# The recurrence's chunk matrices as 64x64 blocks, and the triangular system by 16-blocks and an off-block part

## The reference

```python
def step(state, inp):
    r_t, w_t, k_t, v_t, aa_t, bb_t = inp
    sa = jnp.einsum('bhij,bhj->bhi', state, aa_t)
    state = (state * w_t[:, :, None, :] + sa[..., None] * bb_t[:, :, None, :]
             + v_t[..., None] * k_t[:, :, None, :])
    y = jnp.einsum('bhij,bhj->bhi', state, r_t)
    return state, y
...
xs = (r_h, w_h, k_h, v_h, -kk, kk * a_h)      # kk: k * k_k with each head at norm 1
yn = (y - mu) * lax.rsqrt(var + GN_EPS)       # per head, then gn_w, gn_b
bonus = jnp.sum(r_h * k_h * r_k, axis=-1, keepdims=True) * v_h
out = (yn + bonus) * heads(g)
```

## Time and profile before

| | us |
|---|---|
| device time, median of 3 runs | 3460.9 |
| lowest, highest | 3459.4, 3460.9 |
| span of the profiled execution | 3467.7 |
| the recurrence, units 0 to 7 (2032.6 to 2572.5) | 539.9 |

### The profile page before, as it was taken

How to read it: one execution, slowest core, us unless ns; L and a number is a source line. 1 busy time by engine, 2 the same in 40 slices (tenths; PEclk the granted TensorE clock), 3 DMA queues, 4 the chain that set the end, 5 groups by cost and what they waited for, 6 DMA issues and landing times.

```text
span 3467.7 us, 42391 instructions
## 1 busy us (share of the span) xinstructions
PE 3300.9 (95%) x16430; PEld 2572.9 (74%) x16430; DVE 2089.3 (60%) x3506; ACT 1468.8 (42%) x2635; POOL 0.2 (0%) x4
## 2 busy tenths in 40 slices
PE   8989999999999999999999998898999999999888
PEld 7456666788888877788886677787874788777766
DVE  3535766567666567755555766655544466655665
ACT  2213555553333345533335544444421464554333
POOL 0000000000000000000000000000000000000000
PEclk9999999999999999999997999999999999999999
DMA  6510000232333465433333000000022524455645
GB/s 258 182 43 1 1 1 13 73 104 82 94 114 105 149 215 177 151 110 103 116 100 134 16 19 7 13 26 1 1 82 89 187 95 136 143 175 188 207 159 181
DMA packets 254505, 351.21 MB, mean 101 GB/s; under 512 B 12385, under 2 KB 142049, under 8 KB 251105
## 3 DMA queue, kind: packets, MB, share of 16 engines
q1 hardware_dynamic: 254304, 348.50, 29.9%
HBM read 264.04 MB, written 84.41 MB: 100 GB/s over the span
## 4 chain that ended last, share of the span: by engine, by line
PE 74%; DVE 11%; DMA 8%; issue 3%; ACT 3%; SPq 0%; DVEq 0%; ACTq 0%
PE ps L199 72%; DMA wr<-in_w_down 6%; DVE wl L407 2%; DVE M L3175 1%; DMA hid<-ob 1%; PE ps L1573 1%; DVE NM L2430 1%; PE ps L935 1%; ACT wh L383 1%; DVE Yf L508 0%; DVE ob L1326 0%; DVE QT L2449 0%; DVE RT L2448 0%; DVE QT L2451 0%; PE ps L2868 0%
## 5 line engine op out<-in xcount | busy, mean ns | idle before, releaser
L199 PE MATMUL ps<-ffn_h,wh 128*128 128x512 f32 x2176 | 673.1, 390 | 9.8 <-DVE ob L1326 6.5
L407 DVE TENSOR_TENSOR wl<-wr,wh 128x512 fp32r<-128x512 f32 x610 | 403.1, 687 | 278.4 <-ACT wh L383 275.7
L383 ACT ACTIVATE wh<-wr 128x512 fp32r<-128x512 f32 x610 | 364.5, 625 | 457.3 <-PE ps L199 265.0
L199 PEld LDWEIGHTS ps<-ffn_h,wh 128*128 128x128 f32 x2176 | 408.2, 188 | 99.8 <-DVE ob L1326 10.8
L199 PE MATMUL ps<-ffn_h,wl 128*128 128x512 f32 x1088 | 424.1, 390 | 0.0
L199 PE MATMUL ps<-in_h,wh 128*128 128x512 f32 x1200 | 371.0, 390 | 4.5 <-DVE Yf L837 4.5
L199 PE MATMUL ps<-wh,wh 128*128 128x512 f32 x756 | 302.0, 399 | 40.4 <-DVE wl L407 40.0
L199 PE MATMUL ps<-M,M 128*128 128x128 f32 (+1 forms) x2176 | 293.7, 295 | 37.4 <-DVE ybT L3337 16.6
L199 PEld LDWEIGHTS ps<-M,M 128*128 128x128 f32 (+1 forms) x2176 | 274.5, 200 | 57.1 <-DVE ybT L3337 18.0
L199 PE MATMUL ps<-wl,wh 128*128 128x512 f32 x756 | 299.6, 396 | 0.0
L199 PE MATMUL ps<-wh,wl 128*128 128x512 f32 x756 | 299.3, 396 | 0.0
(11 more groups left out here) (360 smaller groups left out, 5375.5 us busy)
## 6 DMA issues: line engine op xcount, KB each, us to landing
hid<-ob SPq DMA_DIRECT2D x174, 256.0 KB, 2.3
wr<-hid SPq DMA_DIRECT2D x84, 512.0 KB, 4.4
wr<-in_w_down SPq DMA_DIRECT2D x72, 512.0 KB, 3.6
wr<-in_w_up SPq DMA_DIRECT2D x54, 512.0 KB, 4.5
wr<-in_w_in SPq DMA_DIRECT2D x42, 512.0 KB, 5.2
kept<-ob SPq DMA_DIRECT2D x84, 256.0 KB, 2.0
late<-in_w_ada SPq DMA_DIRECT2D x16, 1024.0 KB, 7.4
wr<-in_w_out SPq DMA_DIRECT2D x32, 512.0 KB, 4.3
```

Of the source, the lines that this page charges most:

```text
L199: return e.op.matmul(out, left, right, start=start, stop=stop, skip_group_check=True)
L383: e.op.activation(self.rows(s)[0], src, ACT.Copy).then_inc(*e.event(self.name + "_act", ("w_high", self.name, s)))
L407: e.op.tensor_tensor(lo, src, hi.bitcast(F32), ALU.subtract).then_inc(*e.event(self.name + "_dve", ("w_low", self.name, s), *done))
```

## The change

The matrices of both heads are made in one generator, step by step, as 64x64 blocks without the zero blocks. Position rows of chunk c of a pair (c = 0, 1) are partitions 64 c to 64 c + 63; a tile holds 4 pairs of one head as [128, 4, 64] or two such side by side as [128, 4, 128]. A matmul is 64x64 by 64x64 or by 64x128. In `prod` it reads and writes partitions 64 c; in `pairs` it reads partitions 64 s (channels of head s) and writes 64 c, and four matmuls go over (s, c) = (0,0), (1,1), (0,1), (1,0). At and Rt are one array AR, so n with arb, and ak with ark, become one product each (`nr`, `kr`) under one mask. The a rows and the product akv are one array AV.

The triangular system is solved inside the 16-blocks to X as before; the whole off-block part, G = X^T A_off, is nilpotent after 4 blocks, so (1 + G^2)(1 + G) X replaces the four solves: gt, g, g2, y0, y1, y2 for y0, r1, y1, r2, y2, r3, y3. R2 and Y0 come from one step `out`, MT and NN from one step `state`, for both heads.

Banks are no longer dealt in turn: the chunk uses 0 to 5 by a table, enter 6 (and 7 for rate), leave 7. The decays exp(L - ld) and exp(L_end - L) are no longer made; a shifted view of exp(L) and a product with the chunk's whole decay (GC) stand for them, and the factor -exp(-0.5) moves into the exponentials' scale. `k_end` becomes a product of Kt and GC late in the unit.

```diff
-    def rows_tensor(self, e, j, what, src, ready, lo, hi):
+    def rows_tensor(self, e, j, what, src, ready):
         group = (what, j)
-        bank, free = self.k.bank(group, lo, hi)
+        _, free = self.k.settle(group, 6)
...
-        pairs("a", self.At, self.Bt)
-        pairs("n", self.Bt, self.At)
-        pairs("ak", self.Kt, self.At)
-        prod("a2", "a", "n")
...
+    BANK = {"a": 0, "nr": 2, "kr": 4, "a2": 2, "n2": 0, "a4": 2, "xn4": 0, "x4": 4, "a8": 2, "akv": 0, "x8": 4, "gt": 2, "g": 0, "y0": 4,
+            "g2": 2, "y1": 0, "y2": 4, "out": 2, "state": 4}
+        four_ways = [(u, s, c) for u in range(4) for s, c in ((0, 0), (1, 1), (0, 1), (1, 0))]
+        def pairs(what, left, right, n):
+            for s in range(2):
+                claim(s, what)
+            for u, s, c in four_ways:
+                x = mm(e, k.out(name(s, what), n, n * u, part(c)), left(s, u, c), right(s, u, c), True, True)
...
+        def prod(what, left, right, n, *ready):
+            for s in range(2):
+                claim(s, what, ...)
+                for u in range(4):
+                    for c in range(2):
+                        x = mm(e, k.out(name(s, what), n, n * u, part(c)), left(s)[part(c), u, :], right(s)[part(c), u, :], True, True)
+                done(x, s, what)
...
+        pairs("a", at, bt, 64)
+        pairs("nr", bt, ar, 128)
+        pairs("kr", kt, ar, 128)
+        prod("a2", of(N16), of(A), 64, ("a16", "a"), ("read", "nr"))
+        prod("n2", of(A), of(N16), 64)
+        prod("a4", of(N2), of(A2), 64, ("read", "n2"), ("read", "a2"))
+        prod("xn4", of(A2), of(XN), 128, ("x1", "nr"))
+        prod("x4", of(A), of(X), 64, ("read", "a4"), ("x2", "xn4"))
+        prod("a8", of(N4), of(A), 64, ("read", "xn4"))
+        prod("akv", of(Ak), of(values), 64, ("read", "kr"))
+        prod("x8", of(A2), of(X), 64, ("read", "a8"), ("read", "x4"))
+        prod("gt", of(Aoff), of(X), 64, ("read", "x8"), ("read", "a"))
+        prod("g", of(X), of(Aoff), 64)
+        prod("y0", of(X), of(AV), 128, ("read", "akv"))
+        prod("g2", of(G), of(GT), 64, ("read", "g"), ("read", "gt"))
+        prod("y1", of(GT), of(WU), 128, ("read", "y0"))
+        prod("y2", of(A2), of(WU), 128, ("read", "g2"), ("read", "y1"))
...
-        e.op.tensor_tensor(k_[:, :], k_[:, :], E1[:, :], ALU.mult).then_inc(*done("k_end"))
+        yield
+        yield
+        yield
+        yield
+        e.wait_ge(("kt", j))
+        e.op.tensor_tensor(by_chunk(k_[:, :]), by_chunk(self.Kt[:, sl]), whole, ALU.mult).then_inc(*done("k_end"))
```

More of the change, by code:

```diff
@@ L2823, in columns_of, with enter_tensor @@
         return slice(512 * (j % 2), 512 * (j % 2) + 512)
[L2825 to L2831 removed]
+    def enter_tensor(self, e, j):
         k, hp = self.k, j // 2
         r, k_, v, ld, a_, L, kk, E1, E2, Q1 = self.T
[L2834 removed]
+        for part, what, b in ((0, "decay", 6), (64, "rate", 7)):
             group = (what, j)
[L2836 removed]
+            _, free = k.settle(group, b)
             e.wait_ge(free, "w2", "a2", "tanh", ("shifted", "hidden"))
@@ L2874, in rows_copy @@
-        e.op.activation(dst[:, self.columns_of(j)], self.k.out((what, j)), ACT.Copy).then_inc(*e.event("mix_act", ("read", (what, j))))
-    def rhs_read(self, j):
-        return [("rhs", "chunk", j, s, "rhs") for s in range(2)] if j >= 0 else []
+        src = self.k.out((what, j))
+        e.wait_ge(("mm", (what, j)), self.rows_done(j - 2))
+        if dst is self.AV:
+            dst, src = dst[:, 4 * (j % 2):4 * (j % 2) + 4, :, 0:64], src.rearrange("p (u s n) -> p u s n", u=4, s=2)
+        else:
+            dst = dst[:, self.columns_of(j)]
@@ L2879, in enter_scalar @@
+        e.op.activation(dst, src, ACT.Copy).then_inc(*e.event("mix_act", ("read", (what, j))))
+    RATE = float(np.exp(-0.5))
     def enter_scalar(self, e, j):
@@ new lines, in chunk_scalar, with keep @@
+    def chunk_scalar(self, e, j):
+        k, th = self.k, j % 2
+        A, Aoff, A2, N4, GT, G, NR, KR, XN, WU = zip(*self.mats)
+        name = lambda s, what: ("chunk", j, s, what)
+        def keep(what, dst, a=0, b=64, n=64, after=None):
+            for s in range(2):
+                e.wait_ge(("mm", name(s, what)), (after, name(s, what)) if after else None)
+                e.op.activation(dst(s), self.four(name(s, what), a, b, n), ACT.Copy).then_inc(*e.event("chunk_act", ("read", name(s, what))))
+        for _ in range(3):
+            yield
+        keep("a2", lambda s: A2[s][:, :, :])
+        yield
+        keep("n2", lambda s: XN[s][:, :, 64:128])
+        yield
+        keep("a4", lambda s: A[s][:, :, :])
+        yield
+        keep("xn4", lambda s: N4[s][:, :, :], 64, 128, 128, "x2")
+        yield
+        yield
+        keep("a8", lambda s: A2[s][:, :, :])
+        yield
+        keep("akv", lambda s: self.AV[:, 4 * th:4 * th + 4, s, 64:128])
@@ L3253, in leave_tensor @@
         Yt, yc = self.GN
-        made = [("read", ("chunk", j, s, w)) for s in range(2) for w in ("nn1", "mt1", "r2m", "y0m")]
+        made = [("read", ("chunk", j, c, w)) for c in range(2) for w in ("out", "state")]
+        yield
+        yield
         for i in range(8):
```

551 lines of the change are left out of this document (248 added, 303 removed).

## The result

The changed kernel takes 0.9466 of the time before, 95% interval 0.9447 to 0.9485: 3276.7 us against 3460.9, 184 us less, where 171 were forecast. Two of the changed kernel's four runs took 3391.3 and 3395.4 us and are left out of the ratio; the profile shown here is of the first of them, in which the work ahead of the recurrence ran at a granted clock of 0.50 for 280 us where the profile before has 48. That stretch ends at 2132.1 us, before the recurrence begins at 2134.9; a second profile gives the same eight units within 1 us.

What follows compares the result with a forecast made beforehand. PE bounded the old kernel; afterwards waiting order would. A steady unit: 37 us work, 8.6 stalls and switches, 3.4 clock, about 49. Savings of 131, 18 and 22 make 171, so 3460.9 becomes 3290 us; range 3235 to 3345 (0.8).

Steps and rivals of the forecast that it cites:

- PE's work, 57 to 37 us: Steady recurrence unit at full clock: block products fall from 46.7 to 26.7 us, the remaining 10.3 us stay.
- I take the two that rows show: For a, nr, kr, out and state: two tiles share the array; four sharing, held possible, would save 5 us per unit.
- Rival (1): Four tiles share or the clock holds: a unit of 41 us, 235 us less, 3226 us; chance 0.08.
- rival (2): A product's two tiles don't share because both write one bank: a unit of 61.5 us, 3386 us; chance 0.10, longer queues included.
- The other engines: In a steady unit DVE falls from 42.5 to 32.6 us and ACT from 30.7 to 26 us.
- The walk: One steady unit followed step by step through the engines' queues: 37 us of PE work, 8.6 us of stalls and tile switches.
- Mean's wait: PE's mean step waits for DVE's Yt, queued behind other DVE work: about 1.1 us idle per steady unit.
- a_rows: PE's a-row transposes wait for ACT's v_rows copy out of bank 6, behind y0's evacuations and two table loads: 4.3 us.
- k_rows' 1.2: At the unit's end PE waits 1.2 us for k_end, which DVE does after the MT adds that wait for state.
- The clock, 3.4 us a unit: Half-speed spells follow PE's idle gaps, one after the 4.3 us gap and probably another: 3.4 us added per steady unit.
- Rival (3): Waits spread over the stage keep the clock at 0.50: a unit of 77 us, 52 us more, 3513 us; chance 0.05.
- The sum: Units 1 to 6 at 49 us save 131 us, unit 0 saves 18, unit 7 saves 22: 171 us in all.

Runs made afterwards that it cites:

- norm later and k_rows: Changed kernel with the group norm one step later on ACT and DVE, k_rows in bank 7 and k_end two steps earlier: 0.9309 of the time before.
- norm later: Changed kernel with only the group norm's steps one step later on ACT and DVE: runs of 3231.2 and 3236.5 us.
- half a remedy: Changed kernel with k_rows written to bank 7 in place of 6, k_end left in its place: 0.9458 of the time before.
- no loads: Changed kernel with the group norm's Ln and Exp replaced by copies, so no table loads for them: 0.9343 of the time before.

## Why the prediction held, and where it was off

**PE's work, 57 to 37 us.** Right in its sum, less so in its terms. With the clock at 1.00 throughout (norm later and k_rows) the steady units have 34.9 us of PE in the mean. The step "I take the two that rows show" for a, nr, kr, out and state was the wrong choice of its two ends: four share. These five groups were forecast at 0.93 + 3.58 + 5.8 = 10.3 us; at full clock (norm later, unit 4) they take 0.75, 1.80 and 2.96 from their first record to the next group's, 5.5 in all. So the 5 us held possible are there, 4.8 of them. By the Trainium skill (TensorEngine Tiling (Array Packing), Key Properties) tiles work independently, and the trace agrees. The other work came to 29.4 us where 26.7 stood, among it the five 512-column products, 1.06 us from one start to the next where 0.86 stood; the prediction's "10.3 us" for the rest of the unit is also 9.9 by its own terms. The issue gap, 0.9 us a unit in the mean, was a term that the sum didn't have. Rival (1)'s condition came true, its time did not.

**Sharing within one bank.** Right, and rival (2) fell by the 1.10 us product. The rule that the Trainium skill gives in TensorEngine Tiling (Array Packing) (Restrictions and Gotchas, one bank not for different row tiles at a time) isn't borne out: each head's part of a product writes one bank from both row halves, at 0.028 us a record.

**The other engines.** DVE 29 and ACT 24.5 us against 32.6 and 26 forecast; neither binds.

**The walk.** Mean's wait was 1.1 and is 0.4 to 0.8. **a_rows** waits 4.19 us where 4.3 stood, by exactly the row of work that was named, absent in unit 0. Out's 1.0 is 0.89. k_rows' 1.2 is 1.19; its cause, k_end, was one of two, and the other (b_rows' copy in the same bank 6) came last by the trace. Both had to go.

**The clock, 3.4 us a unit.** The mechanism was right, the size a little too large: a spell behind a_rows in each steady unit (y1 takes 3.0 to 3.7 us in place of 1.96), a second behind k_rows in every other one. PE's time in a steady unit is 37.6 us in the mean against the 34.9 at full clock, 2.7 us; the granted clock with both is 0.89 to 0.96. Rival (3) fell: the level is 1.00 in units 0 and 7 and, with both waits gone, 1.00 in all of the others.

**The sum.** Steady units of 46.1 us in the mean where 49 stood: 18 us of the stage's difference of 21; unit 0 was right (36.6 for 36), unit 7 forecast 3 too long (35.1 for 38). The 2.9 us are PE's work (34.9 for 37: 2.1), the clock (2.7 for 3.4) and the idle time (8.4 for 8.6). That the unit came so near was in part luck: the sharing of four tiles took 4.8 us off, and 2.7 us of other work and the gap put most of that back. "What lies around the stage is left alone" held within the noise. Span for span the forecast is 3297 against 3276, the stage's 21 us; it came out at 13 (3290 for 3277) because the forecast takes from the median a gain that was read from an execution 6.8 us longer.

## What to carry over

When small block matrices are multiplied on a large array, price the records by the tiles that work at once, and then walk one period: this gain was all PE's time on its matmuls, and each further 10 us was in the place of an instruction, not in its work. Look first at what stands behind a slow neighbour in an in-order queue (two table loads ahead of a copy that frees a bank), and count the half-speed stretch behind a wait with the wait. Where a wait names one releaser, ask what would be last without it: here a second was 0.2 us behind, and half a remedy gave nothing.

## What the runs showed of the hardware that was not expected

- Four 64*64 tiles of 64 columns give a record each 0.015 us (0.69 us for 32), below what two give (0.028). In six of the changed kernel's eight units the 192 records of out and state hold a gap of 0.9 to 1.8 us with no releaser and take 4.1 to 5.0 us with it, 21 to 26 ns a record; in the other two they take 2.96 us, 15 ns. By the Trainium skill (TensorE: Matmul & The Clock Gate, Wait — 56ns, not 53.3ns?) starts are never closer than about 25 ns; the units without a gap disagree.
- In the changed kernel the gaps stand where a packet of PE's instructions (256 of them, 16384 bytes, 1.0 to 1.4 us under way) starts 0.9 to 1.7 us into that run of records, and there only. At 0.028 us a record, two tiles at a time, such a packet is followed by no gap.
- Matmuls of a free tile start ahead of earlier ones of a busy tile (2213.75 to 2214.09 above). The same page of the Trainium skill (Part 3, The mechanism) has matmuls start in program order; by these rows that doesn't hold across tiles.
- A wait of 4.2 us was followed by a granted clock of 0.50, 1.2 GHz, in each of six units; with it gone PE's time fell by 15.5 us beside the 23.6 of waiting. A single wait of 1.4 us (no loads) was not. An issue gap and k_rows' 1.2 us stood close together in units 0, 1, 2, 3 and 5, and a spell followed behind 1, 3 and 5 only; with the norm later the same pair stood in four units and a spell followed once. What decides it wasn't settled.
